# RWKV's block joins and triangular solves: matmuls reordered over the column halves of TensorE

## The reference, cut to what matters

```
def step(state, inp):
    r_t, w_t, k_t, v_t, a_t, b_t = inp
    sa = jnp.einsum('bhvk,bhk->bhv', state, a_t)
    state = (state * w_t[:, :, None, :] + sa[..., None] * b_t[:, :, None, :]
             + v_t[..., None] * k_t[:, :, None, :])
    y = jnp.einsum('bhvk,bhk->bhv', state, r_t)
    return state, y
...
_, y = lax.scan(step, state0, seq)
```

## Time and profile before

| | |
|---|---|
| median of 3 runs | 975.17 us (974.79 to 975.6) |
| profiled execution, its own time | 976.25 us |
| span of the profile (first to last instruction) | 974.5 us |
| mean granted TensorE clock | 0.994 of full |
| PE busy | 945.6 us, 97% |
| DVE busy / ACT busy | 643.1 us, 66% / 524.3 us, 54% |

### The profile page before, as it was taken

How to read it: one execution, slowest core, us unless ns; L and a number is a source line. 1 busy time by engine, 2 the same in 40 slices (tenths; PEclk the granted TensorE clock), 3 DMA queues, 4 the chain that set the end, 5 groups by cost and what they waited for, 6 DMA issues and landing times.

```text
span 974.5 us, 19290 instructions
## 1 busy us (share of the span) xinstructions
PE 945.6 (97%) x8533; PEld 916.4 (94%) x8533; DVE 643.1 (66%) x739; ACT 524.3 (54%) x616; POOL 1.1 (0%) x12
## 2 busy tenths in 40 slices
PE   7899999999999999999999988999999999999998
PEld 7899999999999999999899988899889999999998
DVE  2997888874767456566699764446676675466565
ACT  3445453445544569853674652277646644354445
POOL 0000000000000000000000000000000000000000
PEclk9999999999999999999999999999999999999998
DMA  9999457855486443476345442124317356555531
GB/s 339 360 370 320 153 174 259 296 182 174 130 279 197 130 140 121 136 251 186 127 130 172 134 131 81 51 87 148 124 45 237 109 196 217 181 187 195 172 110 44
DMA packets 153438, 172.28 MB, mean 177 GB/s; under 512 B 4000, under 2 KB 137692, under 8 KB 153228
## 3 DMA queue, kind: packets, MB, share of 16 engines
q1 hardware_dynamic: 151696, 167.43, 53.0%
q10 hardware_dynamic: 1660, 3.63, 1.1%
HBM read 170.00 MB, written 1.05 MB: 176 GB/s over the span
## 4 chain that ended last, share of the span: by engine, by line
PE 50%; ACT 4%; DVE 4%; issue 2%; DVEq 0%; ACTq 0%
PE pj L2604 39%; PE m_all L2055 1%; ACT w_hi L951 1%; PE pj L2563 1%; PE pj L2564 1%; PE pj L2565 1%; PE pj L2420 1%; PE m_all L2329 1%; PE m_all L2314 1%; PE m_all L2454 1%; PE m_all L2256 1%; ACT work L1349 0%; DVE work L1874 0%; PE m_all L2481 0%; PE m_all L2359 0%
## 5 line engine op out<-in xcount | busy, mean ns | idle before, releaser
L1455 DVE TENSOR_TENSOR w_lo<-raw,w_hi 128x2048 fp32r<-128x2048 f32 (+1 forms) x126 | 285.6, 2269 | 137.6 <-ACT w_hi L951 136.9
L2604 PE MATMUL pj<-h_hi,w_hi 128*128 128x256 f32 x1224 | 347.4, 284 | 2.9 <-DVE h_lo L1883 1.1
L2604 PE MATMUL pj<-h_lo,w_hi 128*128 128x256 f32 x1224 | 341.8, 279 | 0.0
L2604 PE MATMUL pj<-h_hi,w_lo 128*128 128x256 f32 x1224 | 341.7, 279 | 0.0
L951 ACT ACTIVATE w_hi<-raw 128x2048 fp32r<-128x2048 f32 (+1 forms) x126 | 237.8, 1890 | 53.9 <-PE pj L2604 28.2
L2604 PEld LDWEIGHTS pj<-h_hi,w_hi 128*128 128x128 f32 x1224 | 228.9, 187 | 7.8 <-issue 5.9
L2604 PEld LDWEIGHTS pj<-h_lo,w_hi 128*128 128x128 f32 x1224 | 229.0, 187 | 0.3
L2604 PEld LDWEIGHTS pj<-h_hi,w_lo 128*128 128x128 f32 x1224 | 228.9, 187 | 0.2
L2604 PE MATMUL pj<-y_hi,w_hi 128*128 128x256 f32 x592 | 166.2, 281 | 1.0 <-issue 0.8
L2604 PE MATMUL pj<-y_hi,w_lo 128*128 128x256 f32 x592 | 165.5, 280 | 0.0
L2604 PE MATMUL pj<-y_lo,w_hi 128*128 128x256 f32 x592 | 165.1, 279 | 0.0
(11 more groups left out here) (402 smaller groups left out, 1152.8 us busy)
## 6 DMA issues: line engine op xcount, KB each, us to landing
raw<-in_odd_in_w_dram SPq DMA_DIRECT2D x28, 1024.0 KB, 5.4
raw<-in_w_in_dram SPq DMA_DIRECT2D x23, 1024.0 KB, 5.3
raw<-in_ada_w_dram SPq DMA_DIRECT2D x22, 1024.0 KB, 7.1
raw<-in_w_ff_in_dram SPq DMA_DIRECT2D x16, 1024.0 KB, 5.3
raw<-in_w_ff_out_dram SPq DMA_DIRECT2D x16, 1024.0 KB, 5.2
raw<-in_even_in_w_dram SPq DMA_DIRECT2D x13, 1024.0 KB, 5.2
raw<-in_even_out_w_dram SPq DMA_DIRECT2D x8, 1024.0 KB, 6.5
raw<-in_odd_out_w_dram SPq DMA_DIRECT2D x8, 1024.0 KB, 5.3
```

Source lines behind the costliest of these rows:

```text
L1455: V.tensor_tensor(lo[:, 0:n], raw_of(u)[:, 0:n], hi[:, 0:n].bitcast(F32), ALU.subtract).then_inc(done, 1)
L2604: m = nc.tensor.matmul(to, a_, b_, start=(s == 0 and q == 0 and (fb == 0 or not together)), stop=(s == len(steps_) - 1 and q == 2), skip_g ...
```

## The change

Three steps are reordered. No matmul is added or removed.

1. `rw_join` and `rw_joined` loop over heads outside and chunks inside, and chunk 0 now writes partitions 0 to 63 and chunk 1 partitions 64 to 127, in both steps. Consecutive matmuls so go to different column halves of the array. Both chunks' signals come at the end. ACT's copies read the new places.
2. `rw_joined` waits once for both chunks' first products (`rw_cross` at 4) rather than for one chunk at a time.
3. `solve_u` does the lower and the upper product of a head in turn, where it did all eight lower ones and then all eight upper ones.

```
@@ ScalarE: rw_join, rw_joined
-  nc.scalar.activation(cross_of(c)[RW_B:P, ...], M[2 + c][RW_B:P, :], ACT.Copy)
+  nc.scalar.activation(cross_of(c)[RW_B:P, ...], M[2 + c][tiles[c], :], ACT.Copy)
...
-  nc.scalar.activation(um_of(c)[0:RW_B, ...], M[2 + c][0:RW_B, :], ACT.Copy)
+  nc.scalar.activation(um_of(c)[0:RW_B, ...], M[2 + c][tiles[c], :], ACT.Copy)
@@ TensorE: rw_join
-  for c in range(2):
-      for h in range(RW_H):
-          m = nc.tensor.matmul(M[2 + c][upper_, hcol(h)], cross_of(c)[lower, h, :], t_of(c)[lower, h, :], start=True, stop=True)
-      m.then_inc(S("rw_pairs"), 1)
+  for h in range(RW_H):
+      for c in range(2):
+          m = nc.tensor.matmul(M[2 + c][tiles[c], hcol(h)], cross_of(c)[lower, h, :], t_of(c)[lower, h, :], start=True, stop=True)
+          if h == RW_H - 1:
+              m.then_inc(S("rw_pairs"), 1)
@@ TensorE: rw_joined
-  for c in range(2):
-      pe.wait_ge(S("rw_cross"), 3 + c)
-      for h in range(RW_H):
-          m = nc.tensor.matmul(M[2 + c][lower, hcol(h)], cross_of(c)[upper_, h, :], tt_of(c)[upper_, h, :], start=True, stop=True)
-      m.then_inc(S("rw_pairs"), 1)
+  pe.wait_ge(S("rw_cross"), 4)
+  for h in range(RW_H):
+      for c in range(2):
+          m = nc.tensor.matmul(M[2 + c][tiles[c], hcol(h)], cross_of(c)[upper_, h, :], tt_of(c)[upper_, h, :], start=True, stop=True)
+          if h == RW_H - 1:
+              m.then_inc(S("rw_pairs"), 1)
```

More of the change, by code:

```diff
@@ L1184, in rw_join @@
                     act.wait_ge(S("rw_pairs"), 4 + c)
-                    nc.scalar.activation(cross_of(c)[RW_B:P, :, :].rearrange("p h w -> p (h w)"), M[2 + c][RW_B:P, :], ACT.Copy).then_inc(S("rw_cross"), 1)
+                    nc.scalar.activation(cross_of(c)[RW_B:P, :, :].rearrange("p h w -> p (h w)"), M[2 + c][tiles[c], :], ACT.Copy).then_inc(S("rw_cross"), 1)
                 for c in range(2):
@@ L1192, in rw_joined @@
                     act.wait_ge(S("rw_pairs"), 6 + c)
-                    nc.scalar.activation(um_of(c)[0:RW_B, :, :].rearrange("p h w -> p (h w)"), M[2 + c][0:RW_B, :], ACT.Copy).then_inc(S("rw_cross"), 1)
+                    nc.scalar.activation(um_of(c)[0:RW_B, :, :].rearrange("p h w -> p (h w)"), M[2 + c][tiles[c], :], ACT.Copy).then_inc(S("rw_cross"), 1)
             def solve_w(c):
```

## The result

The changed kernel takes 983.55 us (median of 6 runs, 981.13 to 985.23) where the one before takes 975.95 (6 runs). The ratio is 1.0063, 95% interval 1.0038 to 1.0087: 6.1 us more, 3.7 to 8.5. A second set of runs gives 983.50 against 975.67 and 1.0068 (1.0050 to 1.0086): 6.6 us, 4.9 to 8.4. One execution of `solve0_alone` took 2123.68 us where its others took 975 to 985; it counts as slow and is left out everywhere. The forecast was slower, at 979.2 us in a range up to 981.2. The direction is right; the size is too small and the time lies above the range.

What follows compares the result with a forecast made beforehand. TensorE, its records covering 97% of the span, was taken as the bound. Joins -1.86, waits +0.43 and solves +3.9 made +2.5 us (977.7); one clock fall of 1.5 gave 979.2 us, range 976.5 to 981.2.

Steps and rivals of the forecast that it cites:

- TensorE sets the end: From rw_join to solve_u(1), a microsecond TensorE spends more or less moves the kernel's end by nearly a microsecond.
- The joins, -1.86 us: In rw_join and rw_joined, alternating columns halves each step from 1.86 to 0.93 us, 1.86 us less for two.
- The waits, 0.43 us: Before rw_joined and solve_u(0), two waits for ACT's copies take 0.43 of the 1.86 us; solve_u(0) starts 1.43 us earlier.
- The solves, +1.95 us each: In solve_u, 16 visits of 0.257 us make 4.1 us in place of 2.15, 3.9 us more for both.
- The other rule: In solve_u, changing the tiling mode drains the engine: each of 16 boundaries waits for the array to empty; trace 0.15 us.
- The faster rival: In solve_u, a head's lower and upper products run side by side; a solve takes 1.0 us, total 971.4 us; chance 0.06.
- a boundary of 0.06 to 0.12 us: In solve_u, a shape change cheaper than 0.15 us, or slack further back: sum -1 to +1.9, about 976; chance 0.10.
- The sum by durations, +2.5 us: Joins, waits and both solves together: solve_u(1) ends 2.5 us later, 977.7 us in medians before any clock fall.
- The term for the clock: Behind one of the two solves, one more fall to half clock, 1.5 us, giving 979.2 us; chance 0.36.
- The case with two falls: The same shape-change cost with two more falls of the clock, giving 980.7 us; chance 0.19.

Runs made afterwards that it cites:

- solve0_alone: The kernel before with only the first solve, solve_u(0), alternating lower and upper product per head; ratio 1.0038, 3.7 us above the kernel before.
- full_rows: The whole change, with the lower product also over all 128 rows, upper half of its weights zeroed by VectorE; ratio 0.9971, 2.8 us below the kernel before.
- idle_instead: The kernel before with ScalarE copies repeated, so TensorE waits 1.6 us more before the first solve and 1.9 us behind the second; ratio 1.0061, 6.0 us more.
- full_two_engines: full_rows with ScalarE's upper-block copies moved earlier and VectorE making chunk 1's join copies, to remove its waits; ratio 0.9956, 4.3 us below the kernel before.
- solves_only: The kernel before with the changed solves, joins as before; ratio 1.0063, 6.2 us above the kernel before.
- solves_twos: The kernel before with both solves changing shape after every two heads; ratio 1.0030, 2.9 us above the kernel before.
- solve1_alone: The kernel before with only the second solve, solve_u(1), alternating lower and upper product per head; ratio 1.0030, 2.9 us above the kernel before.

## Why the prediction was right in direction and short in size

**TensorE sets the end.** Right: each stretch that became longer or shorter came out at the end. The shorter ones do so within 0.5 us, the longer ones with more on top.

**The joins, -1.86 us.** Right. Columns alternating under the same 64 rows, which no row before showed, halve the time. The Trainium skill (TensorE: Matmul & The Clock Gate, Packing small matmuls) lets a weight load overlap matmuls in flight only where the row group differs; the trace disagrees, 0.93 us in both joins.

**The waits, 0.43 us.** Somewhat too small. The idle times are 0.19 and 0.32, together 0.51 us. They cost more: `solve_u(0)` starts 4.96 us behind the first join record (608.09 to 613.05) where it was 6.16, so it is 1.20 us earlier and not the forecast 1.43, and 0.66 of the 1.86 us are lost. Part of the rest is an overlap that is gone: in the kernel before, the second join started 0.06 us ahead of the end of `mats` 6 and 7 (609.27 + 1.16 against 610.37), and a step that waits does not. ScalarE's pair of copies out of PSUM takes 1.20 us and not the 1.15 of the pair inside SBUF that I took.

**The solves, +1.95 us each.** 617.13 - 613.05 = 4.08 against 2.15, +1.93, for 4.1 and +1.95 forecast. The way back from 128 by 64 to 64 by 64 costs as much as the way there. The other rule, that a change of tiling mode drains the engine (the Trainium skill, TensorEngine Tiling (Array Packing), Key Properties), agrees with the sign of the result, and the trace gives the price: 0.14 us for each change. The faster rival, both products side by side, is what full_rows shows, once both have one shape. Two limits in the prediction's rivals were worked out wrongly, without a part in the forecast: the sum falls below -1.95 us from a visit of 0.12 us down (2 x (16 x 0.118 - 2.15) - 1.43), not 0.09; and a boundary of 0.06 to 0.12 us, with 0.11 us between a visit's two records, makes the sum -0.3 to +1.6 and not -1 to +1.9.

**The sum by durations, +2.5 us.** It is 4.33 less one fall of 1.66, +2.7: the solves' 2 x 1.93 less the 1.20 of the joins.

**The clock: the step that failed.** The term for the clock, "one more fall", 1.5 us, was too small for what the timed executions show beside the durations. The price of a fall was right, 1.5 us forecast and 1.5 to 1.66 measured, and both profiles of the change have one fall in the stretch. But the sum with one fall left 4.0 us; measured are 6.1 and 6.6, which leave 3.4 and 3.9 us beside the durations, as much as two falls and a bit would cost. By the medians it is more: 983.55 is 4.35 us above the forecast, of which 0.8 is the median of before (975.95 after six runs, 975.17 after three), 0.2 the sum of the durations, and 3.4 what this term lacks, 4.9 us in place of 1.5. In all seven comparisons in which the solves or the waits at them became longer, the time rose by 1.0 to 3.9 us more than the stretch without its falls; in the four in which it became shorter, the two agree within 0.5 us. One by one, this excess is clear of the time's interval only in the two sets of the change and in idle_instead.

I had read the one fall in one profile as the kernel's state. In fact the place of the falls differs between profiled executions, also where the kernels are the same. Between 400 us and the joins, the profile of before falls at 596.6 us alone, those of the change at 580.2 and 597.3 (580.0 and 597.1). Of the nine others six fall between 578.9 and 581.3, five of these again or still between 594 and 601, two at 595 alone, and full_two_engines at 491.6 and 597.5. The fall at 580, which the profile of before lacks, shows in the change's: from the 4500th record of TensorE to the joins it takes 73.4 us against 71.9. The two solves each offer one more place, and both places can be hit in one execution, as idle_instead shows with waits there. The case with two falls was in the prediction at 980.7 us and a chance of 0.19; with the median of before at 975.95 in place of 975.17 it gives 981.5, 2 us under what came.

What stays open is the cause of the 3.4 to 3.9 us. The timed executions have no trace, only a mean clock, and this doesn't carry the whole difference. It is 0.993 over the 68 runs of before for which it is on record, and 0.991 over the 12 of the change. Among the runs of before 0.001 of it goes with some 0.65 us (975.1 us at 0.996, 979.7 at 0.989), so 0.002 explains 1.3 us and 2.1 to 2.6 are left. The mean is a poor count of falls in dense work: the profile of the change has three falls between 580 and 640 us and a mean of 0.995, that of before one there and 0.994, because its clock is at half once in the first 13 us and again in the last 5.8. That two falls behind the solves are the usual case is therefore argued, not shown; shown are falls behind either one, behind both in idle_instead, and their price. A rival was not tested: falls further back. The profiles of solves_only, solves_twos and full_rows have one at 714 to 723 us which before and the change lack, and these three take 340.9 to 341.1 us behind the stretch where before takes 340.24. Whether longer solves make such a fall more frequent, no run shows; full_rows, whose solves are shorter, has it too.

## What to carry to other kernels

Alternating small matmuls over the halves of the array halves their time here (plain fp32, 64x64 and 128x64) as long as all of them use the same shape of it; alternating between shapes costs 0.14 us at each change and turned the gain into a loss. Where two products of different shape must share the array, give both the larger shape with zero weights, or group them by shape. And a single profile shows one placement of the clock's falls: a stretch in which the array has little to do should be priced with falls of its own, here about 1.6 us each, and what durations and falls leave unexplained should be said.

## What the runs showed of the hardware that I had not expected

- The granted clock can fall from 1.00 to 0.50 behind small matmuls that change the shape of the array. In solve1_alone it fell behind a stretch in which TensorE's records cover 2.81 of 3.50 us, and in solves_only behind one that they cover wholly (3.62 of 3.62 us, 31 records). A busy share near 100% in the records did not keep the clock; behind the first solve of the change, 32 records in 4.08 us, it held in both profiles.
- Waiting cost more than its own length: idle_instead stands still for 3.5 us more and loses 6.0 (4.1 to 7.8), with two more falls in its profile.
- ScalarE copies PSUM partitions 0 to 63 into SBUF partitions 64 to 127 at the same pace as straight ones: two in 1.20 us, of 0.6 us each.
